# Gated FFNs with stationary weights: 10 of 11 gate-and-up groups as 256-token products, inner rows not turned

## The reference, cut to what matters

```python
def swiglu(x, w_gate_up, w_down):
    gate, up = jnp.split(x @ w_gate_up, 2, axis=-1)
    return (jax.nn.silu(gate) * up) @ w_down

    ff = swiglu(rms_norm(h, g[0]), ffn_w_gate_up[i, 0], ffn_w_down[i, 0])
    h = h + 0.5 * rms_norm(ff, g[1])
```

## Time and profile before

| | |
|---|---|
| median of three runs | 1620.4 us (1620.27 to 1620.67) |
| profiled execution: span | 1619.2 us; its own time outside the profile is not given |
| PE busy | 1601.9 us (99%), 10213 products and as many loads |
| DVE, ACT, POOL busy | 1010.7 (62%), 875.0 (54%), 135.3 us (8%) |
| DMA | 261.76 MB, mean 162 GB/s |

### The profile page before, as it was taken

How to read it: one execution, slowest core, us unless ns; L and a number is a source line. 1 busy time by engine, 2 the same in 40 slices (tenths; PEclk the granted TensorE clock), 3 DMA queues, 4 the chain that set the end, 5 groups by cost and what they waited for, 6 DMA issues and landing times.

```text
span 1619.2 us, 25752 instructions
## 1 busy us (share of the span) xinstructions
PE 1601.9 (99%) x10213; PEld 1319.1 (81%) x10213; DVE 1010.7 (62%) x1576; ACT 875.0 (54%) x1358; POOL 135.3 (8%) x153
## 2 busy tenths in 40 slices
PE   8999999999999999999999999999999999999999
PEld 7888888888888888887777788888887787788887
DVE  5555576655556555588766576555667845757673
ACT  6454455654446454596555455544558633566662
POOL 2000001000000000024120000000030200001220
PEclk9999999999999999999999999999999999999999
DMA  8665565666556656553322347655553212556552
GB/s 279 184 186 189 182 202 178 193 184 185 189 183 204 185 184 189 187 161 93 92 79 93 105 150 226 183 184 191 155 172 109 92 29 92 169 177 182 175 182 91
DMA packets 209240, 261.76 MB, mean 162 GB/s; under 512 B 21803, under 2 KB 145122, under 8 KB 209122
## 3 DMA queue, kind: packets, MB, share of 16 engines
q1 hardware_dynamic: 208834, 259.60, 51.8%
q10 hardware_dynamic: 288, 0.52, 0.1%
HBM read 259.01 MB, written 1.05 MB: 161 GB/s over the span
## 4 chain that ended last, share of the span: by engine, by line
PE 90%; DVE 5%; ACT 3%; issue 1%; POOL 0%; DVEq 0%; ACTq 0%
PE acc L458 26%; PE acc L460 25%; PE acc L459 25%; DVE low L433 1%; PE tr L716 1%; PE aux L1003 1%; ACT high L423 1%; PE tr L534 1%; PE tr L3567 1%; PE aux L2774 1%; DVE gdn_cv L1453 1%; PE aux L1011 1%; PE aux L1018 0%; PE acc L3152 0%; PE tr L1889 0%
## 5 line engine op out<-in xcount | busy, mean ns | idle before, releaser
L433 DVE TENSOR_TENSOR low<-raw,high 128x1024 fp32r<-128x1024 f32 (+1 forms) x488 | 588.0, 1221 | 382.7 <-ACT high L423 381.7
L423 ACT ACTIVATE high<-raw 128x1024 fp32r<-128x1024 f32 (+1 forms) x488 | 503.8, 1047 | 348.5 <-PE acc L460 339.0
L458 PE MATMUL acc<-high,xh 128*128 128x512 f32 (+1 forms) x1344 | 538.4, 401 | 3.7 <-DVE low L433 3.0
L460 PE MATMUL acc<-high,xl 128*128 128x512 f32 (+1 forms) x1344 | 521.7, 388 | 0.0
L459 PE MATMUL acc<-low,xh 128*128 128x512 f32 (+1 forms) x1344 | 520.3, 387 | 0.0
L458 PEld LDWEIGHTS acc<-high,xh 128*128 128x128 f32 x1344 | 252.5, 188 | 57.4 <-DVE low L433 5.7
L460 PEld LDWEIGHTS acc<-high,xl 128*128 128x128 f32 x1344 | 252.3, 188 | 53.1
L459 PEld LDWEIGHTS acc<-low,xh 128*128 128x128 f32 x1344 | 253.0, 188 | 46.8 <-issue 0.7
L458 PE MATMUL acc<-high,hh 128*128 128x512 f32 x472 | 185.7, 393 | 0.0
L460 PE MATMUL acc<-high,hl 128*128 128x512 f32 x472 | 183.9, 390 | 0.0
L459 PE MATMUL acc<-low,hh 128*128 128x512 f32 x472 | 183.7, 389 | 0.0
(11 more groups left out here) (471 smaller groups left out, 1644.9 us busy)
## 6 DMA issues: line engine op xcount, KB each, us to landing
raw<-in_ffn_w_gate_up SPq DMA_DIRECT2D x350, 256.0 KB, 3.2
raw<-in_ffn_w_down SPq DMA_DIRECT2D x176, 256.0 KB, 3.0
raw<-in_gdn_w_in SPq DMA_DIRECT2D x96, 256.0 KB, 3.0
raw<-in_ffn_up SPq DMA_DIRECT2D x88, 256.0 KB, 3.2
raw<-in_w_in SPq DMA_DIRECT2D x72, 256.0 KB, 2.9
raw<-in_sc_w_in SPq DMA_DIRECT2D x48, 256.0 KB, 3.1
raw<-in_ffn_down SPq DMA_DIRECT2D x44, 256.0 KB, 2.9
raw<-in_gdn_w_out SPq DMA_DIRECT2D x32, 256.0 KB, 3.0
```

The costliest lines, as they stand in the source:

```text
L423: nc.scalar.activation(high[t % HIGHS][:, 0:n], raw[t % RAWS][:, 0:n], ACT.Copy).then_inc(high_ready, 1)
L433: nc.vector.tensor_tensor(low[t % RAWS][:, 0:n], raw[t % RAWS][:, 0:n], high[t % HIGHS][:, 0:n].bitcast(F32), ALU.subtract).then_inc(low_r ...
L458: nc.tensor.matmul(o, a, wh, start=(k0 + kk == 0), stop=False)
L460: mm = nc.tensor.matmul(o, b, wh, start=False, stop=(k0 + kk == k - 1))
```

## The change

In the four gated FFNs the groups 1 to 10 are computed the other way round: the weights are stationary, 128 columns at a time (`c` = 0, 1 gate, 2, 3 up), and all 256 tokens of `xh` or `xl` move. Each of the four column pieces has its own 256 columns of PSUM, so a group takes two pairs of banks (`acc` for odd groups, `tr` and `aux` for even ones). The inner rows come out with the inner width on the partitions, as the down projection wants them, so they are not turned. The factor `prs` now has to lie along the free axis: PE turns it once per FFN (`factors_pe`) and ACT copies it to `rb`. DVE multiplies the gate by `rb` (`gate_dve`), ACT applies silu, DVE multiplies by the up part (`hidden_dve`), which is left without the factor; `peps` carries the factor into the norm's epsilon instead. Group 0 keeps the old form, on the `aux` banks, also without the factor on its up part. Its transposes move from behind group 1 to behind group 1's first tile, and those of the small vectors from before group 1 to behind its third tile, into `tr`. A number of GDN semaphores are merged into two, with the same waits. The diff, cut to its core:

```diff
-        xh = sb("xh", [P, DC, SEQ], F32R)
-        xl = sb("xl", [P, DC, SEQ], F32R)
+        xhl = sb("xhl", [P, 2, DC, SEQ], F32R)
+        xh, xl = xhl[:, 0], xhl[:, 1]
...
-        banks = acc[0] + acc[1]
-        tr = [ctx.enter_context(nc.psum_tensor(f"tr{i}", [P, GW], F32)) for i in range(2)]
-        aux = [ctx.enter_context(nc.psum_tensor(f"aux{i}", [P, GW], F32)) for i in range(2)]
+        pairs = [ctx.enter_context(nc.psum_tensor(n, [P, 2, GW], F32)) for n in ("acc0", "acc1", "tr", "aux")]
+        acc0, acc1, tr, aux = ([p[:, i, :] for i in range(2)] for p in pairs)
+        acc = [acc0, acc1]
+        banks = acc0 + acc1 + aux
...
+            up = g[0] in ("ffn00_up", "ffn01_up", "ffn10_up", "ffn11_up")
+            if up and gi > first[g[0]]:
+                turned_nth[gi] = turned_count
+                turned_count += 1
+                place.append([])
+                if (gi - first[g[0]]) % 2:
+                    on_acc = [turned_count] * 4
+                earlier.append(list(count))
+                continue
+            if up:
+                place.append([4, 5])
...
+            if k0 == 0 and tb == 0 and gi in summed_before:
+                pe.wait_ge(summed, 2 * summed_before[gi])
...
+        def turned_products(pe, gi, two, then={}):
+            k = groups[gi][4]
+            for i, t in enumerate(tiles_of[gi]):
+                if i in then:
+                    then[i]()
+                _, k0, kn = tiles[t]
+                pe.wait_ge(low_ready, t + 1)
+                for c in range(4):
+                    o = two[c // 2][:, c % 2, :]
+                    for kk in range(kn):
+                        cols = slice(kk * GW + c * P, kk * GW + (c + 1) * P)
+                        nc.tensor.matmul(o[:, 0:SEQ], high[t % HIGHS][:, cols], xh[:, k0 + kk, :], start=(k0 + kk == 0), stop=False)
+                        nc.tensor.matmul(o[:, 0:SEQ], high[t % HIGHS][:, cols], xl[:, k0 + kk, :], start=False, stop=False)
+                        mm = nc.tensor.matmul(o[:, 0:SEQ], low[t % RAWS][:, cols], xh[:, k0 + kk, :], start=False, stop=(k0 + kk == k - 1))
+                    if k0 + kn == k and c % 2:
+                        mm.then_inc(acc_ready[c // 2], 1)
+                    elif c == 3:
+                        mm.then_inc(used, 1)
...
+                if s.unscaled is not None:
+                    dve.wait_ge(eps_ready, s.unscaled + 1)
+                nc.vector.tensor_scalar(msq[:, tb:tb + 1], ssq[:, tb, 1:2], ssq[:, tb, 0:1],
+                                        EPS / s.factor ** 2 if s.unscaled is None else peps[:, tb:tb + 1],
...
+        def gate_times_up_unscaled(dve, gi, sil):
+            for tb in range(TB):
+                dve.wait_ge(silu_ready, sil + tb + 1)
+                nc.vector.tensor_tensor(prod[gi % 2][tb][:, 0:256], at_acc(gi, tb)[:, 256:512], gate_s[gi % 2][tb][:, :],
+                                        ALU.mult).then_inc(left(gi, tb), 1)
...
+            def two(self, g):
+                return (pairs[0], pairs[1]) if g % 2 else (pairs[2], pairs[3])
...
+            def factors_pe(self, pe):
+                u = self.unit + 1
+                free_unit(pe, u)
+                pe.wait_ge(pre_rstd, TB * (self.n + 1))
+                for tb in range(TB):
+                    mm = nc.tensor.transpose(tr[u % 2][:, tb * P:(tb + 1) * P], prs[:, tb:tb + 1].broadcast_to([P, P]), ident[:, :])
+                mm.then_inc(tr_ready, 1)
+            def first_turned_pe(self, pe, g):
+                gi = self.up + g
+                if g == 1:
+                    for b in range(4):
+                        if earlier[gi][b]:
+                            pe.wait_ge(acc_free[b], earlier[gi][b])
+                elif g == 2:
+                    for b in (4, 5):
+                        pe.wait_ge(acc_free[b], earlier[gi][b])
+                    last = self.unit + (1 if self.n else 3)
+                    for u in (last - 1, last):
+                        pe.wait_ge(tr_free[u % 2], u // 2 + 1)
+                if g > 2:
+                    pe.wait_ge(summed, 2 * self.groups_done(g - 2))
...
             def pe(self, pe, nxt):
                 first_products(pe, self)
-                if self.n == 0:
-                    rest_of_vec_pe(pe)
                 for g in range(1, FG):
-                    products(pe, self.up + g, xh, xl)
-                    transpose_prod(pe, self.up + g - 1, self.unit + g - 1)
+                    self.first_turned_pe(pe, g)
+                    then = {}
+                    if g == 1:
+                        then = {1: lambda: transpose_prod(pe, self.up, self.unit), 2: lambda: self.factors_pe(pe)}
+                        if self.n == 0:
+                            then[3] = lambda: rest_of_vec_pe(pe, self.unit + 2)
+                    turned_products(pe, self.up + g, self.two(g), then)
 
                 def before(k, tb):
-                    u = self.unit + k // 2
                     if k % 2 == 0 and tb == 0:
-                        pe.wait_ge(tr_free[u % 2], u // 2 + 1)
-                last = lambda: transpose_prod(pe, self.up + FG - 1, self.unit + FG - 1)
-                last_products(pe, self.out, nxt, hh, hl, before, {2: last})
+                        if k == 0:
+                            pe.wait_ge(tr_free[self.unit % 2], self.unit // 2 + 1)
+                        else:
+                            pe.wait_ge(hidden_hl, self.groups_done(k // 2))
+                last_products(pe, self.out, nxt, hh, hl, before)
...
+            def factors_act(self, act):
+                u = self.unit + 1
+                act.wait_ge(tr_ready, u + 1)
+                nc.scalar.activation(rb[:, :], tr[u % 2][:, 0:SEQ], ACT.Copy).then_inc(tr_free[u % 2], 1)
+            def silu_act(self, act, g):
+                act.wait_ge(summed, 2 * self.groups_done(g) - 1)
+                x = sums[g % 2][:, 0:2, :]
+                nc.scalar.activation(x, x, ACT.Silu).then_inc(gate_silu, 1)
+            def place(self, x, g):
+                return x[:, 2 * g:2 * g + 2, :]
+            def high_act(self, act, g):
+                act.wait_ge(summed, 2 * self.groups_done(g))
+                nc.scalar.activation(self.place(hh, g), sums[g % 2][:, 2:4, :], ACT.Copy).then_inc(hidden_hh, 1)
...
             def act(self, act, nxt):
                 rms_known(act, self)
                 for g in range(FG):
-                    stream_act(act, self.up + g)
-                    silu(act, self.up + g)
-                    if g:
-                        hidden_high(act, g - 1, self.unit + g - 1)
-                    if self.n == 0 and g == 0:
-                        rest_of_vec_act(act)
-                high_to(act, tiles_of[self.out][1] + AHEAD)
-                hidden_high(act, FG - 1, self.unit + FG - 1)
+                    gi = self.up + g
+                    ahead = tiles_of[gi][-1] + AHEAD
+                    stream_act(act, gi)
+                    if g == 0:
+                        silu(act, gi)
+                        continue
+                    if g == 1:
+                        hidden_high(act, 0, self.unit)
+                        self.factors_act(act)
+                        if self.n == 0:
+                            rest_of_vec_act(act, self.unit + 2)
+                    self.silu_act(act, g)
+                    high_to(act, ahead + 1)
+                    self.high_act(act, g)
...
+            def unscaled_dve(self, dve):
+                dve.wait_ge(pre_ms, TB * (self.n + 1))
+                nc.vector.tensor_scalar(peps[:, :], pms[:, :], EPS / self.factor ** 2, None, ALU.mult).then_inc(eps_ready, 1)
+            def gate_dve(self, dve, g):
+                if g == 1:
+                    u = self.unit + 1
+                    dve.wait_ge(tr_free[u % 2], u // 2 + 1)
+                dve.wait_ge(acc_ready[0], self.up + g + 1)
+                nc.vector.tensor_tensor(sums[g % 2][:, 0:2, :], self.two(g)[0][:, :, 0:SEQ], rb[:, :].unsqueeze(1).broadcast_to([P, 2, SEQ]),
+                                        ALU.mult).then_inc(summed, 1)
+            def hidden_dve(self, dve, g):
+                dve.wait_ge(acc_ready[1], self.up + g + 1)
+                dve.wait_ge(gate_silu, self.groups_done(g))
+                nc.vector.tensor_tensor(sums[g % 2][:, 2:4, :], self.two(g)[1][:, :, 0:SEQ], sums[g % 2][:, 0:2, :],
+                                        ALU.mult).then_inc(summed, 1)
+            def low_dve(self, dve, g):
+                dve.wait_ge(hidden_hh, self.groups_done(g))
+                nc.vector.tensor_tensor(self.place(hl, g), sums[g % 2][:, 2:4, :], self.place(hh, g).bitcast(F32),
+                                        ALU.subtract).then_inc(hidden_hl, 1)
...
             def dve(self, dve, nxt):
                 rms_known(dve, self)
+                self.unscaled_dve(dve)
                 for g in range(FG):
-                    stream_dve(dve, self.up + g)
```

(69 more changed lines are left out.)

86 lines of the change are left out of this document (36 added, 50 removed).

## The result

The changed kernel took 1650.0 us (median of five runs, 1647.6 to 1651.3) against 1620.4 us before: a ratio of 1.0179 with an interval of 1.0167 to 1.0191, so 1.8% or 29.6 us slower. The forecast was 1642.5, slower, in a range of 1633 to 1650. The direction held; the time lies just at the upper end of the range, 7.5 us above the figure. The profiled execution took 1649.5 us, with a span of 1647.7.

The account below looks back on a forecast made before the run. TensorE (PE), busy 99% of the span, bounds the kernel. Terms 24.6 - 17.8 + 0.9 + 0.4 + 9.5 + 3.3 + 1.2 = +22.1; 1619.2 + 22.1 + 1.2 = 1642.5 us, range 1633 to 1650.

Parts of the forecast that it names:

- Products: Gate-and-up groups on PE: 96 products of 256 columns at 120 ns replace 48 of 512; +24.6 us over 40 groups.
- Transposes: Gated FFNs on PE: 11 sets of four become one, 40 sets saved at 0.444 us each; -17.8 us.
- prs and vec: On PE: turning the prs columns once per FFN, +0.9 us; vec transposes now inside a group, +0.4 us.
- Waits: PE's queue: transposes wait for prod, +9.5 us; vec transposes and third groups wait for the bank, +3.3 and +1.2.
- rival B: PE's clock halves after each of five waits over 2 us, about 1.9 us each; +9, 1652 us; 9%.
- D: Rival: ring of two PSUM pairs binds, each later group waits for summed, 0.3 us each; +11, 1653 us; 4%.
- estimate of 5 us: Cost of the doubled product count on PE by the skill page's N/2.4 + 2.5 ns step; whole sum about 1623.
- Rival A: Not slower: exchanged operands make PE's narrow step half a wide one, 113.6 ns; 1617.9 us; 6%.
- C: Rival: PE's waits aren't there, because prod and hidden_low come sooner; 1628.5 us; 4%.
- DVE and ACT: Per group DVE's 512-column work is 2.07 us in place of 1.56, ACT has one silu and one copy; cost 0.

Follow-up runs that it names:

- e4: Kernel before, each 512-column product in gate-and-up groups 1 to 10 cut into two of 256 with the same stationary operand: 1645.3 us, ratio 1.0151.
- e8: Kernel before, with each transpose of prod made twice into the same columns: 1641.8 us, ratio 1.0129.
- e3: Changed kernel, first group's prod transposes one tile later, its hidden_high and hidden_low ahead of the last two tiles' parts: 1629.7 us, ratio 1.0055.
- e5: Changed kernel, with small filler products on PE before the transposes of prod (9 calls) and of vec (13 calls): 1643.8 us, ratio 1.0142.
- e6: e3 with the last two of the three products exchanged, so the same weights don't come twice in a row: 1629.5 us.
- e7: e3 with high x xh and high x xl made by one product of 512 moving columns, VectorE adding the halves: 1618.9 us, ratio 0.9987.
- e9: e7 with a tile's eight wide products together, then its eight narrow ones, order reversed every second tile: 1614.0 us, ratio 0.9957.
- e2: Changed kernel with the first group's transposes of prod behind two tiles of the next group instead of one: 1636.7 us.

## Why the prediction was right or wrong

- **Products, +24.6: right.** The step is 120 ns, the group 11.52 us, and e4 has the same price, +24.5, with the old operands. So the half-width step read in another stage of the program held for exchanged operands.
- **Transposes, -17.8, and prs and vec, +1.3: right** in the sum. e8 confirms the price of a transpose. e3 has +8.9 for products, transposes and these together, predicted +8.1; the 0.8 between them was not looked into.
- **Waits, +14.0: right.** The four for `prod` show 2.1 to 2.2 us of idle time, to which come the 0.16 us by which PE's last product outlasts its step (0.28 against 0.12), the one for the bank 3.16, the three at the third group's start 0.36 of idle time and a restart. e5 less e3 has 14.1.
- **The clock: the term that the sum lacked.** The sum counted idle time as if it cost only itself. The slower clock was rival B with 9%, at 1.9 us for each of five waits, and with the remark that no idle time of the trace before went over 0.90 us. It came true in part: the clock fell at three of the five waits of the profiled execution, and 5.5 us of its time are lost there, 1.5, 1.5 and 2.5; e5 puts the price at 6.2 to 6.8 us. So the price of one fall was near what B had; the sum held nothing for it. Of the 7.5 us between 1642.5 and 1650.0 this is nearly all; e3's 0.8 is the rest. The page of the Trainium skill that was cited beside this rival ("TensorE: Matmul & The Clock Gate", section "Part 1: The HAM clock gate") has the clock halve after idle time; the trace agrees for three waits and not for the other two. B took its price from the opening, where the first small products go at about half the speed, and called that the lower level. The granted clock from 2 to 5.6 us is 1.00 in the trace before, so its rows don't show that level there; the windows behind the waits do.
- **The range held by luck.** The bounds of the sum itself were 1633 and 1648, and 1650.0 is outside of them. It is covered only because the range was drawn 2 us wider at the top, for a small part of B and D, and the changed kernel's own runs spread over both sides of that end.
- **A slip** without weight: 40 x 0.13 in the prediction's estimate of 5 us should be 40 x 0.12, 48 more products per group at 2.5 ns. The 5 us stay.
- **Rival A** (narrow steps at half the price) is excluded by the step of 120 ns, and e4 and e6 show that neither the exchange nor repeated weights change it; **C** (no waits) is excluded by the trace, **D** (the ring of two pairs) by the 11.52 us of a group, which are 96 steps of 120 ns with no gap.
- **DVE and ACT** cost nothing, as said, and did not even in e7, where DVE has seven operations of 512 columns per group in place of three.

## What to carry to other kernels

Before turning an operand round to save transposes, count the products: here a step has a part of some 13 ns that does not shrink with the columns (2 x 120 - 227), so twice as many products at half the width ate the 17.8 us and 6.8 more. What is moved forward in the queue of the engine that bounds must find its data ready there, because a wait there costs its own time and again, at times, a slower clock behind it. Moving the transposes back by one tile, and the operation that frees their bank forward by two, was worth 20 us (e3). When an operand is split in a high and a low part that lie side by side, one wide product does the work of two narrow ones, at the price of four more operations of DVE per group, for which it had the time here (e9).

## What was not expected of the hardware

- Waits of the same length (2.19 us of idle time, at 321.93 and 514.95), at the same place of the second and the third FFN, brought the clock down in one case and not in the other, within one execution. The wait of 3.16 us for the bank is followed by the lower level in the changed kernel's profile and not in e2's. So such a wait has a price that varies from run to run: the changed kernel spread over 3.6 us, e5 over 1.0, e3 over 0.8.
- The clock need not fall while PE is idle. In the second and the fourth FFN it fell at 323.0 and 1009.0, 1.0 and 1.2 us after the wait for `prod` had ended, with PE at work again. At the wait for the bank it fell 1.1 us before the wait's end.
- At the lower level a narrow product's step was 213 ns. That is twice the 107 ns by which the steps of 512 and 256 columns differ (227 - 120), so the other 13 ns don't show there.
- Small products into a bank that is free held the clock at 1.000 through all five waits.
- Products of 512 and 256 columns that alternate at every product cost more than runs of one width: 11.27 - 11.13 = 0.14 us per group, some 6 ns for each of the 24 pairs of the three tiles in which they do. In e7's first tile, where the width changes every two products, hardly any of it shows (2.79 us against 2.78).
